# One layer of a hybrid decoder: order of the first expert's copies and turns, the 13th weight unit in halves, a later down bias, and the recursion's state products split

## The reference, cut to what matters

```
h = rms_norm(x); p = h @ w_in
y_a, wkv_new, row_new = rwkv7_mix(p[..., :SHIFT_COLS], ...)   # 8 heads x 64, recursion over tokens
y_b, buf_new = conv_mix(p[..., SHIFT_COLS:], ...)             # GLU, causal conv of 31, LayerNorm, swish
x = x + concat(y_a, y_b) @ w_out
h2 = rms_norm(x)
# top 4 of 32 experts, softmax over the four logits
gt = min(xe @ w_gate[e] + b_gate[e], 7); up = clip(xe @ w_up[e] + b_up[e], -7, 7)
y = ((up + 1) * gt * sigmoid(1.702 * gt)) @ w_down[e] + b_down[e]
x = x + sum over a token's experts of gate * y
```

## Time and profile before

| | us |
|---|---|
| median of three runs | 1165.84 |
| the profiled execution's own time | 1165.45 |
| its span, first to last instruction | 1163.6 |
| TensorE busy | 1122.2 (96%) |
| VectorE busy | 529.1 (45%) |
| ScalarE busy | 212.3 (18%) |
| granted TensorE clock, mean | 0.999 |
| moved by DMA | 430.00 MB, mean 370 GB/s |

### The profile page before, as it was taken

The page is one execution under the profiler, slowest core; times in us unless marked ns, Lnnn a source line. Parts: engine busy times, 40 slices in busy tenths (PEclk is TensorE's granted clock), DMA queues, the critical chain, the costliest instruction groups (busy, mean ns, idle before and its releaser), DMA issues.

```text
span 1163.6 us, 16613 instructions
## 1 busy us (share of the span) xinstructions
PE 1122.2 (96%) x6608; PEld 480.4 (41%) x6608; DVE 529.1 (45%) x1123; ACT 212.3 (18%) x433; POOL 34.1 (3%) x47
## 2 busy tenths in 40 slices
PE   9999999999999999999999999999999999999997
PEld 7666786643333333333333333333333333333332
DVE  6999965337333333333333333333333333333333
ACT  3265642221111111111111111111111111110012
POOL 0002412000000000000000000000000000000000
PEclk9999999999999999999999999999999999999999
DMA  9724006999999999999999999999999999999995
GB/s 247 214 86 179 20 16 175 429 392 415 417 427 427 429 428 430 427 429 427 430 429 427 430 427 430 428 429 427 430 427 429 430 426 430 429 429 427 429 421 204
DMA packets 58587, 430.00 MB, mean 370 GB/s; under 512 B 16670, under 2 KB 29390, under 8 KB 34220
## 3 DMA queue, kind: packets, MB, share of 16 engines
q1 hardware_dynamic: 58288, 428.84, 89.7%
q10 hardware_dynamic: 260, 0.61, 0.2%
HBM read 424.92 MB, written 4.48 MB: 369 GB/s over the span
## 4 chain that ended last, share of the span: by engine, by line
PE 53%; DMA 29%; DVE 4%; issue 1%; ACT 1%; DVEq 0%; ACTq 0%
PE bank L2166 35%; DMA ring<-in_w_up_dram 26%; PE bank L2133 5%; DMA arena<-in_w_up_dram 3%; PE bank L2140 2%; PE bank L2086 2%; PE bank L1734 2%; DVE arena L2536 1%; DVE arena L2560 1%; PE bank L1312 1%; PE bank L1271 1%; PE bank L2174 1%; PE bank L2192 1%; PE bank L1320 0%; PE bank L278 0%
## 5 line engine op out<-in xcount | busy, mean ns | idle before, releaser
L2166 PE MATMUL bank<-arena 128*64 128x512 f32 x1540 | 344.2, 594 | 11.4 <-DMA arena<-in_w_up_dram 11.2
L2166 PE MATMUL bank<-ring,arena 128*64 128x512 f32 x1532 | 342.2, 594 | 11.8 <-DMA ring<-in_w_up_dram 11.0
L2166 PEld LDWEIGHTS bank<-arena 128*64 128x64 f32 x1540 | 108.0, 136 | 225.8 <-issue 197.9
L2166 PEld LDWEIGHTS bank<-ring,arena 128*64 128x64 f32 x1532 | 108.0, 137 | 225.2 <-issue 198.0
L2560 DVE TENSOR_TENSOR arena<-arena,bank 128x512 f32<-128x512 f32 x180 | 110.0, 680 | 0.0
L2549 DVE SCALAR_TENSOR_TENSOR arena<-bank,arena 128x512 f32<-128x512 f32 x31 | 23.3, 751 | 182.0 <-ACT arena L1928 182.0
L2536 DVE TENSOR_SCALAR arena<-bank 128x512 f32<-128x512 f32 x31 | 21.4, 692 | 179.9 <-PE bank L2174 179.9
L610 PE MATMUL bank<-arena,ring 128*128 128x336 f32 x352 | 102.5, 447 | 0.3 <-DVE arena L751 0.3
L2133 PE MATMUL bank<-arena 128*64 128x512 f32 x372 | 86.7, 599 | 4.3 <-DVE arena L2560 0.6
L1904 ACT COPY arena<-bank 128x512 f32<-128x512 f32 x31 | 18.2, 587 | 354.3 <-PE bank L2133 354.3
L610 PEld LDWEIGHTS bank<-arena,ring 128*128 128x128 f32 x352 | 65.8, 189 | 34.2 <-issue 2.9
(11 more groups left out here) (387 smaller groups left out, 785.5 us busy)
## 6 DMA issues: line engine op xcount, KB each, us to landing
ring<-in_w_gate_dram SPq DMA_DIRECT2D x32, 2048.0 KB, 29.8
arena<-in_w_up_dram SPq DMA_DIRECT2D x32, 2048.0 KB, 32.8
arena<-in_w_gate_dram SPq DMA_DIRECT2D x32, 2048.0 KB, 29.9
arena<-in_w_down_dram SPq DMA_DIRECT2D x31, 2048.0 KB, 35.4
ring<-in_w_down_dram SPq DMA_DIRECT2D x31, 2048.0 KB, 35.4
ring<-in_w_up_dram SPq DMA_DIRECT2D x29, 2048.0 KB, 32.9
ring<-in_w_in_dram SPq DMA_DIRECT2D x11, 1024.0 KB, 8.4
ring<-in_w_up_dram SPq DMA_DIRECT2D x11, 512.0 KB, 7.3
```

Of the source, the lines that this page charges most:

```text
L2166: mm = M.matmul(bank[64 * hb:64 * hb + 64, b, :], tokens(cc), rows[:, 512 * hb:512 * hb + 512], start=(cc == 0), stop=(w3 == 2 and cc == K ...
```

## The change

In the recursion the eight products with a 64 x 64 identity become one with the 128 x 128 identity, `state` is split into two halves (two products each), of which the second runs in the next round between that identity product and u, VectorE negates u before it adds the sequences' states, and the affine step moves from VectorE to ScalarE, behind `take_v(0)`. For expert 0, `down` comes before the turn of the gates, the turn of the gathered rows stands between the two down units, and ScalarE copies the activation before the rows. Unit 12 is loaded in two halves, the first as soon as half of unit 4 has been used. The down bias goes into the combine of expert 29, in the body of expert 30, instead of that of expert 0.

```
@@ scan_act
+            for j in range(4):                       # behind take_v(0)
+                nc.scalar.activation(zT[:, j, :], zT[:, j, :], ACT.Identity, bias=vecA[:, V_CLB + j:V_CLB + j + 1],
+                                     scale=vecA[:, V_CLW + j:V_CLW + j + 1]).then_inc(S["z_scaled"], 1)
@@ scan_pe
-                    each(4, identity, kept_state, 64, C, True, False)
+                    M.matmul(bank[:, 4, 0:256], ident, Zc.rearrange("p j k -> p (j k)"), start=True, stop=False)
+                    state(c - 1, 1)
...
-                    each(7, lambda i, j: identc, lambda i, j: szb[:, i, j, 0, :], 64, C, True, False)
+                    for i in range(2):
+                        M.matmul(bank1(7)[side(i)], identc, szb[:, i, :, 0, :], start=True, stop=False)
...
-                    state(c)
+                    state(c, 0)
@@ scan_dve
-            z_affine(0)
...
+                dve.wait_ge(S["u_done"], c + 1)
+                negated(c // 2, c % 2, 2).then_inc(S["un_ready"], 1)
+                if c:
                     dve.wait_ge(S["old_read"], c)
                     dve.wait_ge(S["st_done"], c)
...
-                dve.wait_ge(S["u_done"], c + 1)
-                negated(c // 2, c % 2, 2).then_inc(S["un_ready"], 1)
...
-                if c < 3:
-                    z_affine(c + 1)
@@ sync
+                    if k == NSLOT + 4:
+                        w = unit_src(k // EU, k % EU)
+                        sp.wait_ge(first_half, 1)
+                        sp.dma_start(unit_tile(k)[:, 0:2, :], w[:, 0:2, :]).then_inc(half_landed, 16)
+                        sp.wait_ge(unit_used, UPRE + k - NSLOT + 1)
+                        sp.dma_start(unit_tile(k)[:, 2:4, :], w[:, 2:4, :]).then_inc(landed[k % NSLOT], 16)
+                        continue
@@ scalar, body
-                    take_rows(at(1, 3))
-                    take_act(at)
                     if first:
+                        take_act(at)
+                        take_rows(at(1, 3))
                         act.wait_ge(F["gt_turned"], 1)
                         A.copy(gT32, bank[:, 6, 0:NT]).then_inc(F["gt_ready"], 1)
+                    else:
+                        take_rows(at(1, 3))
+                        take_act(at)
@@ tensor, product
+                        if u and between:
+                            between()
+                            if first and k == 4 and c == 2:
+                                mm.then_inc(first_half, 1)
@@ tensor, body
-                        combine(before, biased=second)
+                        if second:
+                            pe.wait_ge(F["gt_ready"], 1)
+                        combine(before, biased=late)
...
                     if first:
+                        down(at, over, first=True, between=turn_next)
                         for k in range(6):           # the turn of the gates, gt_turned
...
-                    if not first:
+                    else:
+                        turn_next()
                         pe.wait_ge(F["cmb_read"], before(6, 4))
-                    down(at, over)
+                        down(at, over)
...
-                    body(NGROUP - 1, r)
+                    body(NGROUP - 1, r, late=True)
```

More of the change, by code:

```diff
@@ L1331, in rows @@
                 return v[64 * i:64 * i + n]
-            def identity(i, j):
-                return ident[side(i), side(i)]
             def chunk(c):
@@ L1382, in scan_pe, with state @@
                  64, C, True, True).then_inc(S["u5_done"], 1)
[L1384 to L1396, removed]
+            def state(j, r):
+                if r == 0:
+                    if j == 0:
+                        pe.wait_ge(S["e_ready"], 4)
+                        pe.wait_ge(S["un5_ready"], 2)
+                    else:
+                        pe.wait_ge(S["sout_ready"], j)
+                for i in range(2):
+                    at = 64 * i + 32 * r
+                    mm = M.matmul(bank[side(r), 6 + i, 0:256], VU[2][at:at + 32, i, 1, j, :],
+                                  KBxx[at:at + 32, j, i], start=True, stop=True)
+                if r == 1:
+                    mm.then_inc(S["st_done"], 1)
             for c in range(5):
@@ L1689, in build @@
         early_landed = lsem("early_landed")
+        first_half = lsem("first_half")
+        half_landed = lsem("half_landed")
         PIECES = {PER - 3: 4, PER - 2: 2, PER - 1: 4}
@@ L2141, in turn, with product @@
                     return mm
-                def product(at, k0, b, tokens, w3, over, final=False, first=False, early=False):
+                def product(at, k0, b, tokens, w3, over, final=False, first=False, early=False, between=None):
                     for u in range(2):
+                        if u and between:
+                            between()
                         k = EU * over[0] + k0 + u
@@ L2162, in product @@
                                 mm.then_inc(first_quarter, 1)
-                            if first and cc == 2:
+                            if first and k == 4 and c == 2:
+                                mm.then_inc(first_half, 1)
+                            if first and w3 == 0 and cc == 2:
                                 pe.wait_ge(F["x_ready"], 2)
@@ L2201, in gate_up, with down @@
                             early=early).then_inc(F["u_done"], 1)
-                def down(at, over, final=False):
+                def down(at, over, final=False, first=False, between=None):
                     if final:
@@ L2208, in down @@
                         pe.wait_ge(F["aT_ready"], at(1, 1))
-                    product(at, 4, 2, lambda cc: aT[:, cc % 4, cc // 4, :], 2, over, final)
+                    product(at, 4, 2, lambda cc: aT[:, cc % 4, cc // 4, :], 2, over, final, first=first, between=between)
                 def add_last(i):
@@ L2280, in last_body, with body @@
                     add_last(2)
-                def body(it, r, first=False, second=False):
+                def body(it, r, first=False, second=False, late=False):
                     at = counter(it, GROUP, r)
@@ L2300, in body, with turn_next @@
                     turn_p(at)
-                    pe.wait_ge(F["xg_ready"], at(1, 3))
-                    turn(xg, 5).then_inc(F["x_done"], 1)
+                    def turn_next():
+                        pe.wait_ge(F["xg_ready"], at(1, 3))
+                        turn(xg, 5).then_inc(F["x_done"], 1)
                     if first:
+                        down(at, over, first=True, between=turn_next)
                         for k in range(6):
@@ L2342, in _ @@
                     body(0, r, first=(r == 0), second=(r == 1))
+                pe.wait_ge(half_landed, 16)
                 with pe.Fori(0, NGROUP - 1) as it:
```

9 lines of the change are left out of this document (2 added, 7 removed).

## The result

The changed kernel takes 1169.68 us, median of six runs (1167.93 to 1172.12); the kernel before took 1165.08 beside it (1163.07 to 1166.95). The ratio is 1.0043, with an interval of 1.0033 to 1.0053: slower by 4.6 us. The forecast was 1168.3, slower by 2.45. The direction held, but the size is nearly twice the forecast's. The time lies 0.1 us inside the range of 1164.8 to 1169.8, and only because the runs before beside it were 0.8 faster than the 1165.84 that the forecast started from; 1165.84 + 4.6 = 1170.4 lies above it. The profiled execution took 1168.02 with a span of 1166.2 (before 1165.45 and 1163.6).

What follows compares the result with a forecast made beforehand. The weight stream was taken to bound the kernel through unit 18's late landing, then bytes and tail. +0.25 + 1.0 - 0.3 there and +1.5 behind the stream gave 1165.84 + 2.45 = 1168.3 us, range 1164.8 to 1169.8.

Steps and rivals of the forecast that it cites:

- What bounds the kernel: Weight stream sets the time; unit 18, last late unit, is late by 0.3 us; its issue follows expert 0's down eviction.
- Part 4: Recursion: half states and fewer identity products save 0.3 us on unit 18's landing, bounds 0.7 saved and 0.4 lost.
- Rival 4: Recursion dearer: shape changes cost 0.1 each, `state` in halves 0.4 twice; +0.5 instead of -0.3, 1169.1 us; chance 0.11.
- Part 2: Order at expert 0: eviction waits behind the gates' turn and copy, +1.0 us on unit 18's issue, bounds 0.7 and 1.2.
- Part 1: 13th unit in halves: hole at 260 us closes, unit 18 doesn't follow, gain handed back; drier queue costs +0.25 us.
- Part 3: Late down bias: worth nothing at expert 1, where TensorE waits anyway; +1.5 us at the end, bounds 1.2 and 1.9.
- The sum: +0.25 + 1.0 - 0.3 on unit 18's landing, +1.5 behind the stream: +2.45 us, 1168.3 us; chance 0.48.

Runs made afterwards that it cites:

- the run with eight: Recursion's part of the change alone on the kernel before, with the eight 64 x 64 identity products kept: 1165.54 us against 1164.37, ratio 1.0009.
- the experts' part: Kernel before with all hunks except the recursion's (unit 12 halved, down before gates' turn, late down bias): 1167.44 us against 1164.42, ratio 1.0020.
- the filler: Six products of the bias' shape at expert 1, overwritten by the combine, added to the kernel before with unit 12 halved, down first, late bias: 1166.03 us against 1164.87.
- the run with the states whole: Kernel before with the recursion's part of the change, but both halves of the states issued together at the round's end: 1163.69 us against 1164.42, ratio 0.9995.
- the one with the bias at expert 1: Kernel before with unit 12 halved and down before the gates' turn, down bias left in expert 0's combine: 1164.66 us against 1164.42, ratio 0.9997.
- the early eviction: Expert 0's down product evicted before the gates are copied; first run with unit 12 halved, down first, bias at expert 1: 1164.70 us against 1164.87.
- the table cut: VectorE's overflow-block table made in two pieces; with whole states and early eviction, early bias 1163.54 us, late bias 1164.61, against 1164.37.

## Why the prediction was right or wrong

**What bounds the kernel** held. Unit 18 is the last unit before which the queue runs dry (295.04 to 302.03 is 7.0 us where a backlog gives 4.9), and behind it only bytes and the tail count. The twenty profiles bear it out: from the landing of unit 18 to the end of the span it is 861.8 to 863.3 us in the thirteen with the bias at expert 1 and 863.8 to 864.9 in the seven with the late bias, whatever else was changed.

**Part 4, the recursion, is the step that failed**: "-0.3, bounds 0.7 and -0.4" was +2.3 us on expert 0's start in the trace and +1.8 in the medians, and its sign of being wrong, rounds longer than 3.9 us, came (4.34). The prediction read "the state's two pairs 0.27 us apart" and priced a half at 0.27 to 0.32. The two groups of records were two records of the same products, and a half costs 0.57 to 0.59 however few it holds. One more group in each of four rounds is 4 x 0.58 = 2.3 us, which is what stands between 15.8 and 13.5 us for the recursion. The large identity product was mis-sized as well, 0.63 instead of the 0.45 worked out from a row of eight like ones behind each other. In the split round that counts, 0.18 in each (the run with eight, 0.7 us less in the median); in the whole round the copy of w hides it. The sign was lost between w and u: the earlier trace rows show some 0.55 us there, in which the identity products were hidden; now 0.63 and 0.58 stand in it, 1.21 us from 170.79 to 172.00, while the half that stays at the round's end costs what the whole did. Rival 4, "state in halves costs 0.4 twice", named the place and was too small. The affine steps on ScalarE cost nothing, as forecast: behind them it still waits 1.02 us for TensorE.

The Trainium skill's page "TensorEngine Tiling (Array Packing)", section "Tiling Modes", says that a change of tiling mode drains TensorE, and the prediction drew from it that the recursion "would be worth 0 or cost a little". The runs are in keeping with it, as the single 128 x 128 product between other shapes took 0.63 and not the 0.45 of the estimate, but they don't show it as the cause of the loss: the whole states change shape as well, and lose nothing.

**Part 2, the order at expert 0**, was right to 0.05 in the trace: the eviction is 3.31 us later, 2.26 of it from the start of expert 0, so 1.05 against the +1.0 worked out. Its row of ScalarE in time shows the reason given, the copy of the gates waiting for their turn in front of the eviction:

```profile
266.99 0.44 ACT L1959 COPY arena<-bank 128x336 f32<-128x336 f32 x1 [8.02 <-PE bank L2324]
```

**Part 1, the 13th unit.** Unit 17 landed 0.7 us (292.5 was forecast) to 1.3 us earlier than 295.25 in the two profiles of the experts' part without the filler, at 294.50 and 293.91, and only 0.2 earlier in the changed kernel, where the recursion moved the units between by 2.3 us. The charge of +0.25 us for a drier queue has the wrong sign: unit 18 took 9.9 us before, 8.2 in the changed kernel and about 7.6 in the three runs of the experts' part with the old order of eviction and table. The landings fit one estimate: unit 18 lands 4.9 us behind unit 17 or 7.6 us behind its own issue, whichever is later. For the kernel before that is 300.2 or 298.2 (300.4 in the trace), for the run with the states whole 298.9 or 297.7 (298.85), for the one with the bias at expert 1 298.8 or 299.8 (299.77), for the changed kernel 299.9 or 301.5 (302.03). It holds to 0.6 us in sixteen of the twenty profiles. In the other four, all among the seven with the early eviction, unit 18 lands 1.3 to 2.7 us later than it gives; why is open. By this estimate, where the prediction said "late by 0.3 us only, but it is late", unit 18's issue had some 2 us to spare. An issue that is 3.3 later then costs 1.6, and parts 1 and 2 together, forecast at +1.25, cost 0.2 in the medians, not distinct from nothing.

**Part 3, the late bias**, was right in the tail: from the last landing of an up unit to the end of the last expert's down products it is 18.42 us instead of 16.94, +1.5 as worked out, with the wait for the transfer gone from the chain. It was wrong at expert 1. "This only lengthens that wait", worth nothing, holds for the work and not for the clock: with a wait of 2.65 us instead of 0.61 the granted clock fell in one profiled execution of the three that have this wait, and the medians show 2.8 us for the late bias, 1.5 in the tail and, as what is left, some 1.3 here. The run with the filler and the one with the bias at expert 1 show that the 1.3 belongs to the missing work; that the clock is how, is argued. That the filler gives 1.9 of the 3.0 back, and that with the table cut the late bias costs 1.1, both point there. What share of the executions fall, why the profile of the changed kernel itself kept its clock through the same wait, and why three profiles fell at 145 us without one, is open.

**The sum** of the trace looks right by luck: +2.6 us of span against +2.45, since the recursion's +2.3 instead of -0.3 and unit 18's shorter flight, -1.7 instead of +0.25, cancel; the stream between unit 18 and the last up unit then took 0.6 less, against 1.5 more in the tail. In the medians it is +1.8 (recursion), +2.8 (late bias) and +0.2 (parts 1 and 2), 4.8 for the 4.6 measured. The sum failed by the recursion's 2.1 us and the 1.3 that the late bias cost at expert 1, less the 1.1 that parts 1 and 2 did not cost.

## What to carry to other kernels

Before a group of small products is split, find out whether its records lie behind one another or side by side: where they began 7 ns apart, as here, the group cost one product, and splitting it doubled the price. Price an operation from a row in which it stands as it will stand, alone between other shapes and not in a run of its like. And work that leaves an engine which waits anyway isn't free of effect: look how long the wait becomes, and at the clock granted behind it.

## What the runs showed of the hardware

- A float32 product of 32 rows and 256 columns takes 0.57 us from the group before it to the group behind, four of them on four sets of rows 0.59.
- A float32 product of 128 x 128 x 256 alone between other shapes takes 0.63 us, eight of 64 x 64 x 64 0.45.
- Behind a wait of 2.65 us of TensorE the granted clock was 0.5 for 3.41 us in one profiled execution (from 284.61 us) and stayed at 1.00 in those of two other kernels with the same wait. In three profiles it fell for as long at 145.4 us, where TensorE had not waited since 131 us.
- A transfer of 2 MB issued when the one ahead had 4.7 us left took 9.9 us to land; issued when it had 0.5 to 2 us left (six profiles), 7.6 to 8.2; with 2.6 to 2.9 left (five profiles), anything from 7.7 to 10.3.
